# Four neighbouring rows of the down weights on a partition, gate and up columns in steps of four, and an output projection split in two

## The chip, the core and the metric

The kernel runs on one core of a Trainium2 chip. The core has a matrix engine (TensorE, in the profile PE for its matmuls and PEld for its loads of the stationary operand), a vector engine (VectorE, DVE), a scalar engine (ScalarE, ACT), GpSimd (POOL), and SyncE (SP), which in this kernel issues nearly all transfers. Each runs its own list of instructions in order and waits on semaphores for the others. Sixteen DMA engines move data between the chip's memory (HBM) and the on-chip memory (SBUF, 128 partitions); matmuls write to PSUM. The metric is the time of one execution on the device, in microseconds, as the median over several runs.

## What is computed

A trunk of two layers over 256 tokens of width 1024, all in float32. Layer 0 mixes the tokens with a short gated convolution and a stick-breaking attention; layer 1 with a Mamba-2 mixer (inner width 2048, 32 heads, 8 groups). After each of the two, and this is what most of the change touches, comes a mixture of experts: each token chooses one of 4 groups of experts and in it the best 2 of 8, and 32 experts in all work on the tokens that chose them:

```python
def expert_block(args):
    xb, e = args
    hb = jax.nn.silu(xb @ w_gate[e]) * (xb @ w_up[e])
    return hb @ w_down[e]
```

`w_gate[e]` and `w_up[e]` are 1024 x 512, `w_down[e]` is 512 x 1024: 2 MB (2,097,152 bytes) each, 6 MB per expert, 192 matrices in two layers, some 400 MB that must come from HBM once. A final norm follows. The sum over the 512 inner columns in `hb @ w_down[e]` may be taken in any order, as long as column i of `hb` meets row i of `w_down`.

## The kernel before

**The expert loop.** Each expert gets room for 32 tokens (CAP); tokens beyond that go to an overflow pass, here one in layer 1 and none in layer 0. Experts are worked off in fours (QUAD): for each four, `gather_quad` collects the tokens with matmuls (line 1393), and VectorE scales them. For each expert TensorE runs `gate_up` (line 1402), ScalarE and VectorE form silu(gate) x up, TensorE transposes the result (line 1485), `down` (line 1411) multiplies with the down weights, and every four experts `combine_quad` (line 1421) adds their outputs to four PSUM banks (`acc`). `rows_of` (line 1380) spreads the routing for one expert.

In `gate_up` the 32 tokens are the stationary operand, and the weights move through: the 512 columns of gate and up are cut into four blocks, and block j of both (2 x 128 columns) goes to the partitions 32j to 32j+31 of the PSUM tile. Before the change block j is the 128 neighbouring columns from 128j on. After the transposition the inner index within a block lies on the 128 partitions, so `down` wants row 128j + p of `w_down` on partition p, in the j-th place; there the load before puts it, with the access pattern `"a (j p) n -> p (a j) n"` (line 297, and 316 in the overflow pass). On a partition that is four runs of 1024 floats (4 KB) from four places in HBM. The gate and up loads (lines 294 and 313) put 8 neighbouring rows of 512 floats on a partition, one run of 16 KB.

**Order of the loads.** All are issued by SP. There are three sets of weight buffers (`SLOT`); buffers of slot 0, 1 and 2 are `w_gu[s]` and `w_dn[s]`, of which one pair lies in the tiles named w_x and arena in the profile. The first three experts' weights are loaded before the loop. From expert 3 on, `expert_stream` issues gate, up and down of expert e: the gate load waits until `gate_up` of the expert that used the slot last is done (`gu_done`), the down load until its `down` is done (`dn_done`). At expert 28 `overflow_weights` loads the overflow experts' weights, if there are any, and at expert 30 SP waits for the overflow pass to be done.

**The Mamba layer.** It runs over 8 units g. TensorE's order in a unit is `odd_scores(g)`, `odd_z(g)` (projection of z), `odd_y(g)`, `odd_out(g - 2)` (output projection, four PSUM banks b of 8 matmuls each), `odd_x(g + 1)` (projection of x for the next unit), `odd_ss(g)` (sum of squares for the norm), `odd_bc(g + 2)`. For unit 6 the last of these doesn't exist. VectorE's order for a unit is written out too: `odd_mean(g - 1)`, which waits for `odd_ss(g - 1)`; `odd_x_taps(g)`, the convolution of x, which waits for ScalarE's first tap; `odd_mix(g - 1)`; `odd_x_silu(g)`, for which `odd_scores(g)` waits. ScalarE's order is `odd_x_tap(g)`, `odd_rstd(g - 1)`, `odd_x(g)`. `odd_x(g + 1)` on TensorE waits for `z1_silu` of unit g, since both use the PSUM tile pb. The output projection's semaphore `oproj` frees the buffer `w_o` for SP's load of the next unit's output weights (`rows_odd`, lines 280 and 276) and the buffer `mix1` for VectorE.

Of the kernel before, what the change touches and what calls it, by code (L numbers as in the profile page):

```python
# [12 lines left out]
P = 128  # L13
# [5 lines left out]
ODD_UNITS = 8  # L19
# [8 lines left out]
FF = 512  # L28
QUAD = 4
CAP = 32  # L30
OV_AT = 28
OV_SLOT = 1
# [14 lines left out]
def previous(e):  # L47

    return max(i for i in range(e) if SLOT[i] == SLOT[e])
# [36 lines left out]
def trunk_program(nc, x, even_w_in, even_conv_w, even_w_out, odd_in_proj, odd_conv_w, odd_conv_b,  # L86
# [3 lines left out]
    with ExitStack() as ctx:  # L90
        def sb(name, shape, dt=F32):
            return ctx.enter_context(nc.sbuf_tensor(name, shape, dt))
# [12 lines left out]
        w_gu = [sb(f"w_gu{s}", [P, 2, KC, FF]) for s in range(2)]  # L105
        w_dn = [sb(f"w_dn{s}", [P, FF // P, D]) for s in range(2)]
# [78 lines left out]
        mix1 = [take(2, SEQ) for _ in range(2)]  # L185
# [74 lines left out]
        def _(sp_):  # L260
# [27 lines left out]
            def expert_part(l, e, part, after=None):  # L288
                s = SLOT[e]
                if after is not None:  # L290
                    sp_.wait_ge(S["dn_done" if part == 2 else "gu_done"], after + 1)
                w = (expert_w_gate, expert_w_up, expert_w_down)[part][l, ds(e, 1), :, :]
                if part < 2:
                    sp_.dma_start(w_gu[s][:, part], w.rearrange("a (p k) f -> p (a k) f", k=KC)  # L294
                                  ).then_inc((S["gu_in0"], S["gu_in1"], S["gu_in2"])[s], 16)
                else:
                    sp_.dma_start(w_dn[s][:, :, :], w.rearrange("a (j p) n -> p (a j) n", p=P)
                                  ).then_inc((S["dn_in0"], S["dn_in1"], S["dn_in2"])[s], 16)

            def overflow_weights(l):  # L300

                sp_.wait_ge(S["table_done"], l + 1)
                sp_.wait_ge(S["gu_done"], NE * l + previous(OV_AT + 2) + 1)
                sp_.wait_ge(S["dn_done"], NE * l + previous(OV_AT + 2) + 1)
                k0 = sp_.value_load(table[0:1, l:l + 1], min_val=0, max_val=OV_LIST)
                k1 = sp_.value_load(table[0:1, l + 1:l + 2], min_val=0, max_val=OV_LIST)
                with sp_.If(k0 < k1):
                    with sp_.Fori(k0, k1) as k:
                        sp_.wait_ge(S["ov_done"], k + 1)
                        e = sp_.value_load(table[0:1, ds(k + 3, 1)], min_val=0, max_val=NE - 1)  # L310
                        for part in range(2):
                            w = (expert_w_gate, expert_w_up)[part][l, ds(e, 1), :, :]
                            sp_.dma_start(w_gu[OV_SLOT][:, part], w.rearrange("a (p k) f -> p (a k) f", k=KC)
                                          ).then_inc(S["ov_in"], 16)
                        w = expert_w_down[l, ds(e, 1), :, :]
                        sp_.dma_start(w_dn[OV_SLOT][:, :, :], w.rearrange("a (j p) n -> p (a j) n", p=P)
                                      ).then_inc(S["ov_in"], 16)

            def expert_stream(l):
# [824 lines left out]
        def _(pe):  # L1144
            mm = nc.tensor.matmul
# [15 lines left out]
            def project(dst, w, j, used=None):  # L1161

                for k in range(KC):
                    ins = mm(dst, w[:, k, j, :], hnT[:, k, :], start=(k == 0), stop=(k == KC - 1))  # L1164
                return ins
# [8 lines left out]
            def square_sum(a, last=False):  # L1174
                return mm(wa[0:NG + NE + 1, 0:SEQ], esum[:, :], a, start=False, stop=last, skip_group_check=True)

            def out_project(m, u):
                last = u == ODD_UNITS - 1
                w = w_o
                if u == ODD_UNITS - 2:  # L1180
                    pe.wait_ge(S["wo6_in"], 16)
                    w = w_o6
                else:
                    pe.wait_ge(S["wo_in"], (u + 1 - last) * 16)
                for b in range(4):
                    for i in range(2):
                        for j in range(2):
                            ins = mm(acc[:, b, 256 * i:256 * i + 256], w[:, j, 256 * b + P * i:256 * b + P * i + P],  # L1188
                                     m[:, j, :], start=False, stop=False, skip_group_check=True)
                    if last:  # L1190
                        ins.then_inc(S["eo"], 1)
                        if b:
                            logits_of(1, b - 1)
                if not last:
                    ins.then_inc(S["oproj"], 1)

            pe.wait_ge(S["consts_pool"], 1)
# [2 lines left out]
            for t in range(TT):  # L1200
                pe.wait_ge((S["x_in0"], S["x_in1"])[t], 16)
                for b in range(2):
                    for j in range(4):
                        k = 4 * b + j
                        ins = nc.tensor.transpose(BANKS[2 * t + b][:, P * j:P * j + P], squares[:, t, P * k:P * k + P],
                                                  ident[:, :])
# [190 lines left out]
            def gate_up(xb, c0, s, gu, halves=None):  # L1397
                for k in range(KC):
                    if halves is not None and k % (KC // 2) == 0:
                        pe.wait_ge(S["xs_done"], halves + k // (KC // 2) + 1)  # L1400
                    for j in range(4):
                        ins = mm(gu[32 * j:32 * j + 32, :, :], xb[:, k, c0:c0 + CAP], w_gu[s][:, :, k, P * j:P * j + P],  # L1402
                                 start=(k == 0), stop=(k == KC - 1))
                return ins

# [105 lines left out]
            def odd_x(g):  # L1511
                pe.wait_ge(S["c1_in"], g * 16 + 16)
                if g:
                    pe.wait_ge(S["z1_silu"], g)
                project(pb[:, 0:SEQ], w_c[1], 0)
                project(pb[:, SEQ:], w_c[1], 1).then_inc(S["x1_done"], 1)
# [7 lines left out]
            for k in range(KC):  # L1524
                if k % 2 == 0:
                    pe.wait_ge(S["sq_part"], 5 + k // 2)
                ins = mm(wb[0:1, 0:SEQ], esum[:, NG + NE:], hsq[:, k, :], start=(k == 0), stop=(k == KC - 1))
            ins.then_inc(S["ss_done"], 1)
            pe.wait_ge(S["ss_copied"], 1)
            for t in range(TT):  # L1530
                ins = mm(wa[:, t:t + 1], msR[:, P * t:P * t + P], one_c[0:1, :], start=True, stop=True)
            ins.then_inc(S["ss_t"], 1)
            pe.wait_ge(S["rstd"], 2)
            for t in range(TT):
                ins = mm(pb[:, P * t:P * t + P], st[:, 4, t:t + 1].to_broadcast([P, P]), ident[:, :], start=True, stop=True)
# [41 lines left out]
            def odd_ss(g):  # L1577
                pe.wait_ge(S["yz_done"], g + 1)
                for j in range(2):
                    ins = mm(wb[:, 0:SEQ], ones[:, :], sq[:, j, :], start=(j == 0), stop=(j == 1))  # L1580
                ins.then_inc(S["yss_done"], 1)

            def odd_out(g):
                pe.wait_ge(S["mix1_done"], g + 1)
                out_project(mix1[g % 2], g)

            for g in range(ODD_UNITS):
                odd_scores(g)
                odd_z(g)
                odd_y(g)  # L1590
                if g >= 2:
                    odd_out(g - 2)
                if g + 1 < ODD_UNITS:
                    odd_x(g + 1)
                odd_ss(g)
                if g + 2 < ODD_UNITS:
                    odd_bc(g + 2)
# [29 lines left out]
```

## Time and profile before

| | |
|---|---|
| median of 3 runs | 1404.64 us (1402.79 to 1407.19) |
| the profiled execution: time | 1403.31 us |
| its span, first to last instruction | 1401.2 us |
| TensorE matmuls busy | 1093.9 us (78%), 9381 records |
| VectorE / ScalarE busy | 434.8 us (31%) / 262.1 us (19%) |
| read from HBM | 465.68 MB |
| mean granted TensorE clock | 0.869 of full speed |

A float32 matmul shows as two records. Busy shares are averages over stages of different kinds, so the views by stretch say more: the page's slices, the windows, and the chain of waits, which goes back from the last instruction from each step to what released it. A transfer's piece in that chain runs from its issue to its landing, and in between the transfers queued before it are moved too.

### The profile page before, as it was taken

The numbers are of one execution on the slowest core, as the hardware profiler recorded it, in microseconds if no ns is written. First come the engines' busy times: TensorE is split into PE (matmuls) and PEld (weight loads), VectorE is DVE, ScalarE is ACT, GpSimd is POOL, SyncE is SP. The second block draws the span as 40 slices with busy tenths as digits, with TensorE's granted clock in tenths as the row PEclk, the third lists the DMA queues.
The fourth block names the chain that finished last, engine by engine and source line by source line (L and its number), as shares of the span: only waits on it lengthen the run. The fifth ranks groups of instructions, "written<-read, shape, count | busy, mean of one in ns | idle before, by whom it ended". The sixth has DMA issues, their size and how long they took to land.

```text
span 1401.2 us, 21348 instructions
## 1 busy us (share of the span) xinstructions
PE 1093.9 (78%) x9381; PEld 731.6 (52%) x9384; DVE 434.8 (31%) x1098; ACT 262.1 (19%) x621; POOL 6.9 (0%) x28
## 2 busy tenths in 40 slices
PE   8999786677658677679999998878667576676775
PEld 7888543443424244248888887644334242343532
DVE  2241442212212122224655554452112122222123
ACT  2210111111111111113433323211111111111112
POOL 1000000000000000000000000000000000000000
PEclk9999997978879778879999999989788787878878
DMA  9753599999999999954567652469999999999993
GB/s 345 233 221 153 238 420 423 420 420 423 419 420 422 420 420 418 417 181 124 193 225 241 228 193 98 189 265 419 419 423 420 420 423 420 419 422 420 420 410 161
DMA packets 112901, 468.16 MB, mean 334 GB/s; under 512 B 16940, under 2 KB 56104, under 8 KB 96168
## 3 DMA queue, kind: packets, MB, share of 16 engines
q1 hardware_dynamic: 112304, 466.11, 83.4%
q8 instruction: 76, 1.25, 0.4%
q10 hardware_dynamic: 504, 0.67, 0.1%
q14 instruction: 17, 0.14, 0.0%
HBM read 465.68 MB, written 1.08 MB: 333 GB/s over the span
## 4 chain that ended last, share of the span: by engine, by line
PE 40%; issue 36%; DMA 17%; SPq 3%; DVE 2%; ACT 1%; POOL 0%; DVEq 0%; POOLq 0%; ACTq 0%
DMA w_gu<-in_expert_w_up 15%; PE pb L1164 10%; PE pa L1164 7%; PE acc L1188 4%; PE pa L1402 4%; SPq L294 3%; DMA w_x<-in_expert_w_up 2%; PE wa L1402 2%; PE acc L1290 2%; PE wb L1411 2%; PE pb L1393 2%; PE pb L1219 1%; ACT arena L448 1%; PE wa L1171 1%; PE acc L1421 1%
## 5 line engine op out<-in xcount | busy, mean ns | idle before, releaser
L1402 PE MATMUL pa<-w_gu,arena 128*32 128x256 f32 x1536 | 131.2, 516 | 80.4 <-DMA w_gu<-in_expert_w_up 80.4
L959 DVE TENSOR_SCALAR arena<-arena 128x128 f32<-128x128 f32 x64 | 14.5, 227 | 501.6 <-ACT arena L448 501.6
L448 ACT ACTIVATE arena<-wb 32x256 f32<-32x256 f32 (+3 forms) x327 | 116.8, 357 | 230.2 <-PE wb L1485 124.6
L1402 PE MATMUL wa<-w_gu,arena 128*32 128x256 f32 x1344 | 101.2, 468 | 53.6 <-DMA w_gu<-in_expert_w_up 52.0
L1402 PEld LDWEIGHTS pa<-w_gu,arena 128*32 128x32 f32 x1536 | 61.3, 147 | 144.7 <-DMA w_gu<-in_expert_w_up 85.5
L1164 PE MATMUL pb<-hnT,w_x 128*128 128x256 f32 x512 | 113.7, 380 | 2.4 <-DVE arena L999 2.4
L1164 PEld LDWEIGHTS pb<-hnT,w_x 128*128 128x128 f32 x512 | 96.9, 191 | 15.7 <-issue 2.8
L1402 PEld LDWEIGHTS wa<-w_gu,arena 128*32 128x32 f32 x1344 | 49.0, 134 | 99.9 <-DMA w_gu<-in_expert_w_up 54.4
L1393 PE MATMUL pb<-arena,hs 128*128 128x128 f32 x480 | 74.4, 319 | 31.8 <-issue 15.1
L1393 PEld LDWEIGHTS pb<-arena,hs 128*128 128x128 f32 x480 | 68.5, 227 | 45.9 <-issue 41.2
L1411 PE MATMUL wb<-w_dn,arena 128*32 128x256 f32 x1440 | 87.0, 383 | 2.2 <-ACT arena L448 2.2
L1380 PE MATMUL pb<-arena 32*128 32x512 f32 x128 | 73.6, 655 | 6.2 <-DVE arena L897 6.2
L1402 PE MATMUL wa<-w_x,arena 128*32 128x256 f32 x768 | 54.6, 444 | 26.9 <-DMA w_x<-in_expert_w_up 23.7
L448 ACT ACTIVATE arena<-pa 128x128 f32<-128x128 f32 (+1 forms) x40 | 11.6, 298 | 340.5 <-PE pa L1402 316.2
L448 ACT ACTIVATE arena<-arena 128x512 f32<-128x512 f32 (+5 forms) x85 | 51.4, 623 | 75.9 <-DVE arena L1053 24.3
L1402 PE MATMUL pa<-w_x,arena 128*32 128x256 f32 x512 | 40.7, 487 | 30.7 <-DMA w_x<-in_expert_w_up 30.7
L1411 PEld LDWEIGHTS wb<-w_dn,arena 128*32 128x32 f32 x1440 | 45.6, 111 | 35.2 <-issue 3.9
L1421 PE MATMUL acc<-arena 128*128 128x256 f32 x256 | 58.4, 381 | 6.6 <-ACT arena L448 6.6
L960 DVE RECIPROCAL arena<-arena 128x128 f32<-128x128 f32 x64 | 61.0, 953 | 2.2
L1164 PE MATMUL pa<-hnT,w_x 128*128 128x256 f32 x256 | 59.5, 393 | 0.0
L448 ACT ACTIVATE arena<-wa 128x128 f32<-128x128 f32 (+3 forms) x40 | 12.3, 306 | 250.9 <-PE wa L1402 243.5
L920 DVE TENSOR_SCALAR arena<-pb,slot_id 128x256 f32<-128x256 f32 x64 | 30.9, 483 | 87.8 <-PE acc L1421 60.6
(278 smaller groups left out, 1216.0 us busy)
## 6 DMA issues: line engine op xcount, KB each, us to landing
w_dn<-in_expert_w_down SPq DMA_DIRECT2D x45, 2048.0 KB, 27.3
w_gu<-in_expert_w_gate SPq DMA_DIRECT2D x45, 2048.0 KB, 31.5
w_gu<-in_expert_w_up SPq DMA_DIRECT2D x45, 2048.0 KB, 30.6
arena<-in_expert_w_down SPq DMA_DIRECT2D x20, 2048.0 KB, 27.7
w_x<-in_expert_w_gate SPq DMA_DIRECT2D x20, 2048.0 KB, 32.0
w_x<-in_expert_w_up SPq DMA_DIRECT2D x20, 2048.0 KB, 30.5
w_x<-in_odd_in_proj SPq DMA_DIRECT2D x16, 1024.0 KB, 5.4
w_x<-in_odd_in_proj SPq DMA_DIRECT2D x16, 512.0 KB, 5.5
```

Of the source, the lines that this page charges most:

```text
L294: sp_.dma_start(w_gu[s][:, part], w.rearrange("a (p k) f -> p (a k) f", k=KC)).then_inc((S["gu_in0"], S["gu_in1"], S["gu_in2"])[s], 16)
L448: return nc.scalar.activation(*a, **k)
L920: link(v.tensor_scalar(G4[b], B_ps[:, 0:SEQ], slot_id[:, :], None, ALU.is_equal))
L960: link(v.reciprocal(eg, eg))
L1164: ins = mm(dst, w[:, k, j, :], hnT[:, k, :], start=(k == 0), stop=(k == KC - 1))
L1188: ins = mm(acc[:, b, 256 * i:256 * i + 256], w[:, j, 256 * b + P * i:256 * b + P * i + P], m[:, j, :], start=False, stop=False, skip_group ...
L1290: ins = mm(acc[:, b, 256 * i:256 * i + 256], we_o[:, j, 256 * b + P * i:256 * b + P * i + P], mixA[:, j, :], start=(j == order[0]), stop=( ...
L1380: mm(B_ps[:, :], sel, PG, start=True, stop=True).then_inc(S["b_done"], 1)
L1393: ins = mm(xg[:, k, :], hs[:, t, KC // 2 * half + k, :], quad_slots[:, t, :], start=(t == 0), stop=(t == TT - 1))
L1402: ins = mm(gu[32 * j:32 * j + 32, :, :], xb[:, k, c0:c0 + CAP], w_gu[s][:, :, k, P * j:P * j + P], start=(k == 0), stop=(k == KC - 1))
L1411: ins = mm(Y_ps[32 * c:32 * c + 32, :], ht[:, 32 * j:32 * j + 32], w_dn[s][:, j, 256 * b:256 * b + 256], start=(j == 0), stop=(j == 3))
L1421: ins = mm(acc[:, b, 256 * i:256 * i + 256], a, m, start=False, stop=False, skip_group_check=True)
```

## The change

The down weights' load puts four neighbouring rows (4p to 4p+3) on partition p, in the places j = 0 to 3, so that 16 KB of a partition lie together in HBM. To match it, `gate_up` takes for block j the columns j, j+4, j+8, ... instead of 128 neighbours; the moving operand's floats then lie 16 bytes apart. All counts and shapes of instructions stay. Apart from this, in the Mamba layer the output projection that runs in unit 6 (that of unit 4) does bank 0 ahead of the x projection of unit 7 and banks 1 to 3 behind it.

```diff
--- before.py
+++ after.py
@@ -294,7 +294,7 @@
                     sp_.dma_start(w_gu[s][:, part], w.rearrange("a (p k) f -> p (a k) f", k=KC)
                                   ).then_inc((S["gu_in0"], S["gu_in1"], S["gu_in2"])[s], 16)
                 else:
-                    sp_.dma_start(w_dn[s][:, :, :], w.rearrange("a (j p) n -> p (a j) n", p=P)
+                    sp_.dma_start(w_dn[s][:, :, :], w.rearrange("a (p j) n -> p (a j) n", p=P)
                                   ).then_inc((S["dn_in0"], S["dn_in1"], S["dn_in2"])[s], 16)
 
             def overflow_weights(l):
@@ -313,7 +313,7 @@
                             sp_.dma_start(w_gu[OV_SLOT][:, part], w.rearrange("a (p k) f -> p (a k) f", k=KC)
                                           ).then_inc(S["ov_in"], 16)
                         w = expert_w_down[l, ds(e, 1), :, :]
-                        sp_.dma_start(w_dn[OV_SLOT][:, :, :], w.rearrange("a (j p) n -> p (a j) n", p=P)
+                        sp_.dma_start(w_dn[OV_SLOT][:, :, :], w.rearrange("a (p j) n -> p (a j) n", p=P)
                                       ).then_inc(S["ov_in"], 16)
 
             def expert_stream(l):
@@ -1174,7 +1174,7 @@
             def square_sum(a, last=False):
                 return mm(wa[0:NG + NE + 1, 0:SEQ], esum[:, :], a, start=False, stop=last, skip_group_check=True)
 
-            def out_project(m, u):
+            def out_project(m, u, banks=(0, 1, 2, 3)):
                 last = u == ODD_UNITS - 1
                 w = w_o
                 if u == ODD_UNITS - 2:
@@ -1182,7 +1182,7 @@
                     w = w_o6
                 else:
                     pe.wait_ge(S["wo_in"], (u + 1 - last) * 16)
-                for b in range(4):
+                for b in banks:
                     for i in range(2):
                         for j in range(2):
                             ins = mm(acc[:, b, 256 * i:256 * i + 256], w[:, j, 256 * b + P * i:256 * b + P * i + P],
@@ -1191,7 +1191,7 @@
                         ins.then_inc(S["eo"], 1)
                         if b:
                             logits_of(1, b - 1)
-                if not last:
+                if not last and 3 in banks:
                     ins.then_inc(S["oproj"], 1)
 
             pe.wait_ge(S["consts_pool"], 1)
@@ -1399,7 +1399,7 @@
                     if halves is not None and k % (KC // 2) == 0:
                         pe.wait_ge(S["xs_done"], halves + k // (KC // 2) + 1)
                     for j in range(4):
-                        ins = mm(gu[32 * j:32 * j + 32, :, :], xb[:, k, c0:c0 + CAP], w_gu[s][:, :, k, P * j:P * j + P],
+                        ins = mm(gu[32 * j:32 * j + 32, :, :], xb[:, k, c0:c0 + CAP], w_gu[s][:, :, k, j:FF:4],
                                  start=(k == 0), stop=(k == KC - 1))
                 return ins
 
@@ -1580,18 +1580,22 @@
                     ins = mm(wb[:, 0:SEQ], ones[:, :], sq[:, j, :], start=(j == 0), stop=(j == 1))
                 ins.then_inc(S["yss_done"], 1)
 
-            def odd_out(g):
+            def odd_out(g, banks=(0, 1, 2, 3)):
                 pe.wait_ge(S["mix1_done"], g + 1)
-                out_project(mix1[g % 2], g)
+                out_project(mix1[g % 2], g, banks)
 
             for g in range(ODD_UNITS):
                 odd_scores(g)
                 odd_z(g)
                 odd_y(g)
-                if g >= 2:
+                if g == ODD_UNITS - 2:
+                    odd_out(g - 2, (0,))
+                elif g >= 2:
                     odd_out(g - 2)
                 if g + 1 < ODD_UNITS:
                     odd_x(g + 1)
+                if g == ODD_UNITS - 2:
+                    odd_out(g - 2, (1, 2, 3))
                 odd_ss(g)
                 if g + 2 < ODD_UNITS:
                     odd_bc(g + 2)
```

## Rows read from the trace of the kernel before

**Rows 1.** Page, part 2: transfer rate in 40 slices; packets by size.

```profile
GB/s 345 233 221 153 238 420 423 420 420 423 419 420 422 420 420 418 417 181 124 193 225 241 228 193 98 189 265 419 419 423 420 420 423 420 419 422 420 420 410 161
...
DMA packets 112901, 468.16 MB, mean 334 GB/s; under 512 B 16940, under 2 KB 56104, under 8 KB 96168
```

**Rows 2.** Chain of waits, 200 to 610 us: start us, length us, what.

```profile
206.33 30.60 DMA w_gu<-in_expert_w_up
...
575.17 23.80 DMA w_gu<-in_expert_w_up
```

**Rows 3.** Timeline, TensorE, layer 1's first experts: start us, us, engine, line, xrecords.

```profile
921.03 3.66 PE L1402 MATMUL wa<-w_gu,arena 128*32 128x256 f32 x64
...
959.90 0.42 PE L1402 MATMUL wa<-w_gu,arena 128*32 128x256 f32 x4
```

**Rows 4.** Windows: stretch, us, TensorE busy (records), granted clock, DMA share, GB/s.

```profile
177.00:179.00 2.00, 1.70 (x32) 1.00 1.02 412
192.00:194.00 2.00, 0.92 (x4) 1.00 1.03 414
207.00:209.00 2.00, 2.00 (x11) 1.00 1.04 414
222.00:224.00 2.00, 2.00 (x24) 0.50 1.03 412
237.00:239.00 2.00, 2.00 (x20) 0.50 1.02 410
183.00:189.00 6.00, 6.00 (x55) 0.56 1.00 426
198.00:203.00 5.00, 5.00 (x87) 1.00 1.01 426
212.00:218.00 6.00, 4.20 (x58) 1.00 1.01 431
227.00:233.00 6.00, 3.54 (x43) 0.97 1.01 429
242.00:248.00 6.00, 4.92 (x59) 0.93 0.99 418
300.00:550.00 250.00, 174.94 (x1872) 0.80 1.01 420
```

**Rows 5.** Timeline, TensorE, last two experts of layer 1; [wait before].

```profile
1360.13 6.47 PE L1402 MATMUL wa<-w_gu,arena 128*32 128x256 f32 x64 [2.26 <-DMA w_gu<-in_expert_w_up]
...
1375.07 5.83 PE L1402 MATMUL pa<-w_gu,arena 128*32 128x256 f32 x64 [4.75 <-DMA w_gu<-in_expert_w_up]
```

**Rows 6.** Timeline, SP: gate loads of experts 3 and 30 in layer 1.

```profile
924.75 0.34 SPq L294 DMA_DIRECT2D w_gu<-in_expert_w_gate  x1
...
1344.36 0.33 SPq L294 DMA_DIRECT2D w_gu<-in_expert_w_gate  x1
```

**Rows 7.** Line 1402, gate and up products: duration ns min/median/max.

```profile
L1402 PE MATMUL wa<-w_gu,arena x1344: 379/379/637, 159.8 to 1366.2; 128*32 128x256 f32 x192
```

**Rows 8.** Lines 703 and 883, reductions on VectorE: duration ns min/median/max.

```profile
L703 DVE TENSOR_REDUCE arena<-hnT x2: 1979/1980/1981, 131.6 to 897.8; 128x256 f32<-128x1024 f32 x2
...
L883 DVE TENSOR_REDUCE arena<-hnT x2: 1222/1222/1222, 176.5 to 937.8; 128x32 f32<-128x1024 f32 x2
```

**Rows 9.** Timelines around the x projection of unit 7, by engine.

```profile
843.17 7.17 PE L1188 MATMUL acc<-arena,w_x 128*128 128x256 f32 x32
850.18 7.07 PE L1164 MATMUL pb<-hnT,w_x 128*128 128x256 f32 x32
857.09 1.03 PE L1580 MATMUL wb<-arena,ones 128*128 128x256 f32 x4
...
857.29 1.02 ACT L448 ACTIVATE arena<-pb,vec_cols,conv_cols_sb 128x256 f32<-128x256 f32 x2 [6.80 <-PE pb L1164]
...
858.15 0.42 DVE L1096 TENSOR_SCALAR arena<-wb 128x256 f32<-128x256 f32 x1 [9.27 <-PE wb L1580]
...
864.37 1.19 PE L1559 MATMUL wa<-arena 128*128 128x256 f32 x2 [6.25 <-DVE arena L1017]
```

## The prediction

> **What bounds the kernel now.** I read the page's slices of DMA rate first. In slices 6 to 17 and again in 28 to 39 the transfers run at 410 to 423 GB/s, and between them, in the Mamba layer, at about half of that [rows 1]. The two flat stretches are the two expert loops. Then the chain of waits: through an expert loop it is, every three experts, one piece of some 30.5 us that stands for weight transfers, with a few us of TensorE before it; the last such piece of layer 0 ends at 599.0 [rows 2]. So each loop is bound by the stream of weights, three loads of 2.097 MB per expert. TensorE follows: four experts without a wait take 38.9 us (921.03 to 959.90, [rows 3]), while their twelve loads take 12 x 2.097 MB / 420 GB/s = 59.9 us [rows 4]. It waits for the gate and up weights before nearly each expert, and the last wait of layer 1 is 4.75 us before the gate-up product at 1375.07 [rows 5]. The Mamba layer is bound by TensorE and by the chain of vector and scalar work between its products, not by transfers.
>
> **Part 1, the down weights.** Before, a partition's 16 KB of a down load are four runs of 4 KB from four places in the tensor. After, they are one run of 16 KB, as the gate and up loads have always been. What a packet costs at either size follows from windows that lie within one kind of load. DMA share and GB/s there count the same packets, so their ratio, times 16 engines, times the packet's bytes, is the mean duration of a packet, and it doesn't depend on where the window cuts. Five windows within down loads (the first five rows, one per expert, 15 us apart): 1.02/412, 1.03/414, 1.04/414, 1.03/412, 1.02/410, mean 0.002493; times 16 x 4096 B: 163.4 ns for 4 KB. Five within gate and up loads (the next five): 1.00/426, 1.01/426, 1.01/431, 1.01/429, 0.99/418, mean 0.002357; times 16 x 16384 B: 617.8 ns for 16 KB [rows 4]. Each of 16 engines fills 8 partitions: a down load costs it 32 x 163.4 = 5.229 us, a gate load 8 x 617.8 = 4.943 us. The change turns the first into the second: 0.286 us less per down load.
>
> How many of these lie on the path? Layer 1: the first load of the loop is issued at 924.75, the last up load has landed at 1375.07 [rows 5, 6]; in between run 60 gate and up loads (experts 3 to 31 and one overflow expert) and 29 down loads (experts 3 to 30 and the overflow expert; that of expert 31 comes behind the last up load). 60 x 4.943 + 29 x 5.229 = 448.2 us, against 450.3 measured: about 2 us for the first bytes and the last receipt, so there is no gap to fill, and any saving of a packet moves the end. Layer 0 has no overflow expert: 28 down loads. Sum: 57 x 0.286 = 16.3 us. Bounds: the plain rates of the same windows are 412.4 and 426.0 GB/s, 5.085 and 4.923 us, 0.162 per load, which is 9 us. Upwards, the two steadiest gate windows (431 and 429) as the rate of the whole stream against its 420 give 2.3% of 885 us, 20 us: rates dip at the borders between the two kinds of load, and those borders lose their reason. I take 16.3, since the ratio is free of the cut and its sum meets the measured length.
>
> The page "DMA: Bandwidth & Descriptors" of the Trainium skill, section "Why small descriptors are slow", puts a fixed overhead of about 3 cycles on a packet. An estimate from that: 4 x (128 + 3) against 512 + 3 beats, 1.7% of a down load, 5 us for the 57. The trace shows 5.5% between the sizes, and the measurement decides.
>
> What is late next? Still the stream: an expert's three loads then need 14.8 us, TensorE 38.9 / 4 = 9.7. At the end the last down load must be there when expert 31's product wants it; it lands one load behind the last up load, some 5 us, and the gate-up product (5.83, [rows 5]) and the transpose come first. The place where TensorE could take over is the overflow expert of layer 1: expert 30's gate and up loads are issued at 1344.36 [rows 6] when it is finished, and used at 1360.13 [rows 5], 15.8 us later; two loads take 9.9 and about 1.5 for the latency, so about 4.4 us of older loads were still queued. The three down loads of that stretch take 0.9 of it. 3.5 remain, so the whole saving passes.
>
> **Part 2, gate and up columns in steps of four.** Per gate-up product the number, shapes and stationary tiles of the matmuls stay; only the moving operand now takes every fourth float (16 bytes apart) where it took neighbours. No matmul of the trace before reads its moving operand so. What the rows show: 64 records of 379 ns in 3.66 us [rows 3, 7], so one every 52 ns ((3.66 - 0.38) / 63), on four column tiles side by side. Below, nothing excludes a small gain, but nothing offers one: 0. Above, the nearest reading of floats that aren't neighbours is VectorE's: the reduction of 1024 elements with a step of 1 KB takes 1.98 us, one over 1024 neighbours 1.22, a ratio of 1.62 [rows 8]. The far bound is a fetch of 16 bytes for each float instead of for four: a ratio of 4. I take 1.0: with four tiles side by side a tile has 4 x 52 = 208 ns for the 256 floats of a record, 0.8 ns for each, which leaves two clocks for a float at the granted clock of 1.0 (2.4 GHz), and a slower reading is hidden up to a point: four products may grow by 59.9 - 1.1 - 38.9 = 19.9 us in all, a ratio of 1 + 19.9 / 14.6 = 2.36, before TensorE sets the pace.
>
> What isn't hidden at a ratio r: the first gate-up product of each layer (the first refill waits for it, 3.66 x (r - 1)); the last one of each layer, which starts when its weights land (5.83 us at the lower clock: from hardly anything, if the reading takes a fixed time that the slow pace covers, to 5.83 x (r - 1)); and in layer 1 the two products before the overflow expert is done (the same bounds each, less the 3.5 us above). At 1.62: 4.5 + 0.2 to 7.2 + 0 to 3.7, so 5 to 15 us, middle 10. At 2: 7.3 + 0 to 11.7 + 0 to 8.2, middle 17.
>
> The page "SBUF — State Buffer" of the Trainium skill, section "Specifications", speaks against this edit: lines are 16 bytes, full bandwidth needs at least two hits per line, and each access that crosses to a new line pays. With neighbours a line is hit four times, with the new step once. By that rule the ratio is above 1; it gives no size. It is the rule behind the second and third case below; no row here shows a matmul under it.
>
> **Part 3, the output projection of unit 4 split around the x projection of unit 7.** In the stretch before, the projection takes 7.1 us from 843.17, the x projection runs from 850.18, the sum of squares of unit 6 from 857.09, and then TensorE waits 6.25 us until 864.37 [rows 9]. With one bank of four ahead, the x projection starts at about 845.0 and ends at 851.9, 5.3 us earlier; ScalarE's first tap (857.29 before) follows it. But VectorE's next instruction is the mean of unit 6, at 858.15, released by the sum of squares; the taps of unit 7 stand behind it in VectorE's order, and the scores wait for those. The sum of squares keeps its place behind all four banks, at 857.1, so the mean, the taps and the scores come when they came. Gain 0. Cost: the semaphore that frees the output weights rises 7 us later, at 857.2, so SP's load of unit 5's output weights and, queued behind it, that of unit 6's start 7 us later; they are wanted only after the scores of unit 7 and a z projection of 7 us, behind 871, and a load of that size takes some 5. Behind those in SP's queue stands expert 2's gate load, which waits for the z projection of unit 7 anyway. 0, with 0.2 us either way for one more change of tile on TensorE.
>
> **Sum.** 16.3 + 0 + 0. From the profiled execution's own 1403.3 us (span 1401.2 and 2.1 around it) to 1387.0; that execution lies 1.3 us under the median of 1404.64, so the median to be expected is 1388.3.
>
> **The rivals.** (B) The strided reading costs about what VectorE's does: ratio 1.62, 10 us back, 1398. For it: the row and the rule. Against: another engine, a step of 1 KB, and TensorE's pace per float is slower. (C) The other side: the reading becomes the bound of the gate-up product, ratio 2 to 4. At 2 it gives back 17 us, 1405, which is the point from which the change is a loss. Beyond 2.36 TensorE paces the loop. At 4 a product takes 14.6 us, four experts 82.8 instead of 58.8, over some 15 such groups in both layers +360, and the time is about 1750. For it: four column tiles read at once, 256 floats each, and each float on a line of its own. Against: none of the rows shows reading as TensorE's limit. (D) The packets don't matter: the down loads are limited by what they read or write, and the stream stays at 420 GB/s; 1404.6. Against: two kinds of load, same bytes per partition, same source speed, differ by packet size alone in what the trace shows. (E) The split works: the scores of unit 7 come up to 5.3 us earlier, 1383. Only if VectorE's order weren't what holds them.
>
> **Chances.** Forecast 0.57, B 0.14, C 0.15, D 0.10, E 0.04. A measurement of this kernel can tell about 0.3% (4.2 us) from no change. Faster: 0.565 + 0.13 + 0.02 of C near 2 + 0.02 of D + 0.04 = 0.77. Same: 0.005 + 0.01 + 0.01 + 0.07 = 0.10. Slower: 0.12 of C and 0.01 of D, 0.13. The range runs from 1382 (the 20 us bound of part 1 and a little) to 1405 (B's whole width, C at 2, and most of D); it leaves out C beyond 2.
>
> **What would show it.** Right: the page counts about 65 x 384 = 25,000 fewer packets, those of 8 KB and more grow from 16,733 (112,901 - 96,168, [rows 1]) to some 25,000; rate slices of the loops rise from 420 to about 427; pieces of about 30.5 us in the chain shrink to about 30, gate-up products stay at 3.66 us where nothing interrupts them; the scores of unit 7 keep their 6 us wait. Wrong in part 2: gate-up products of 5.9 us or 7 and more at the full clock, or the wait for weights gone and the rate slices below 420. Wrong in part 1: fewer packets and the same 420. Wrong in part 3: TensorE's wait before the scores of unit 7 at about 1 us.

## Result, and the profile after

The changed kernel takes 1413.38 us (median of 9 runs, 1411.29 to 1417.86) against 1404.64 us before (9 runs, 1402.38 to 1407.33): 0.67% slower, ratio 1.0067 with a 95% interval of 1.0052 to 1.0082. Forecast were 1388.3 us and a range from 1382 to 1405. One execution of E9 below took 1515.01 us at a mean granted clock of 0.704, where the other five took 1380.75 to 1382.84, and is left out of its ratio.

The page after, answering to [rows 1]: span; TensorE; granted clock in tenths and transfer rate in 40 slices of 35.3 us; packets.

```profile
span 1410.8 us, 21349 instructions
...
PE 1251.8 (89%) x9381; PEld 735.3 (52%) x9384; DVE 434.7 (31%) x1098; ACT 262.2 (19%) x621; POOL 6.9 (0%) x28
...
PEclk9999899999899998989999999999999999999899
...
GB/s 344 237 211 155 193 405 427 427 428 426 427 427 427 427 427 415 386 179 143 188 240 233 227 173 110 191 201 427 428 427 426 427 428 426 427 426 427 429 359 143
DMA packets 87940, 468.14 MB, mean 332 GB/s; under 512 B 16940, under 2 KB 56104, under 8 KB 62888
```

The load's part did what it should: 25,000 packets fewer, and the slices of the expert loops stand at 426 to 429 GB/s where they stood at 417 to 423. But the rate sags at the loops' first slices (193 and 405, against 238 and 420) and last ones (386 and 359, against 417 and 410), and TensorE is busy for 1252 us instead of 1094. The gate-up products, answering to [rows 7], and two windows inside one such product each, one at the full granted clock (1.00, 2.4 GHz) and one at the lower (0.50, 1.2 GHz):

```profile
L1402 PE MATMUL wa<-w_gu,arena x1344: 612/632/676, 160.8 to 1378.8; 128*32 128x256 f32 x192
...
L1402 PE MATMUL pa<-w_gu,arena x1536: 616/632/672, 170.8 to 1389.9; 128*32 128x256 f32 x192
```
```profile
420.90:424.30 3.40, 3.38 (x32) 0.50 1.00 424
301.90:309.00 7.10, 7.10 (x64) 1.00 1.01 432
```

Every record now takes 632 ns, at least 612, where it took 379 in the stretches of full clock; and the granted clock no longer matters: 32 records touch 3.4 us of the slow window, 64 touch 7.1 us of the fast one, about the same pace. Before, durations of some 634 ns stood at the lower clock alone (the records that touch 222.0 to 224.0, at 0.50). A product of 64 records takes 7.43 us, where it took 3.66 at the full clock, a ratio of 2.03; behind a wait for weights, where the clock before was partly at its lower level, it took 4.96 to 6.62 and now takes 7.43 to 7.58 too.

Where that reaches the end: the last experts of layer 1 in the timeline of TensorE, answering to [rows 5], and SP's first refills of layer 0.

```profile
1350.67 7.43 PE L1402 MATMUL wa<-w_x,arena 128*32 128x256 f32 x64
...
1360.86 7.50 PE L1402 MATMUL pa<-w_gu,arena 128*32 128x256 f32 x64
...
1371.98 7.43 PE L1402 MATMUL wa<-w_gu,arena 128*32 128x256 f32 x64
...
1383.06 7.45 PE L1402 MATMUL pa<-w_gu,arena 128*32 128x256 f32 x64
```
```profile
168.33 0.33 SPq L294 DMA_DIRECT2D w_gu<-in_expert_w_gate  x1
168.70 0.43 SPq L294 DMA_DIRECT2D w_gu<-in_expert_w_up  x1
180.04 0.33 SPq L297 DMA_DIRECT2D w_dn<-in_expert_w_down  x1
```

No product waits for weights at the end: the starts are 11.1 us apart (1360.86, 1371.98, 1383.06), which is TensorE's own pace for one expert. The stream no longer bounds the last four experts (28 to 31; the overflow expert comes before them). At the start the first refill is issued when the first product is done (160.83 + 7.43), and the second only at 180.04, 11.7 us later, while the two loads of the first take about 10.

The first window below, within the second wait of SP, shows the transfers running dry; two long windows in the middle show the full rate:

```profile
179.00:182.00 3.00, 2.39 (x27) 1.00 0.71 213
300.00:550.00 250.00, 211.62 (x1877) 0.92 1.00 426
1000.00:1250.00 250.00, 218.04 (x1919) 0.92 1.01 427
```

The Mamba stretch, answering to [rows 9]:

```profile
847.40 7.07 PE L1164 MATMUL pb<-hnT,w_x 128*128 128x256 f32 x32
...
859.49 1.03 PE L1580 MATMUL wb<-arena,ones 128*128 128x256 f32 x4
866.77 1.19 PE L1559 MATMUL wa<-arena 128*128 128x256 f32 x2 [6.25 <-DVE arena L1017]
```
```profile
860.55 0.42 DVE L1096 TENSOR_SCALAR arena<-wb 128x256 f32<-128x256 f32 x1 [9.28 <-PE wb L1580]
```

The x projection now starts at 847.40, behind one bank of the output projection (845.57) instead of four, and the wait before the scores of unit 7 is 6.25 us, to the digit what it was: VectorE's mean at 860.55 is still released by the sum of squares at 859.49.

### The profile page after: what moved, and what is told of

Its sections match the earlier page's. It is cut to its first block, busy times and chain, and to the rows that moved or that the text cites. A ratio compares the mean times of both kernels' runs of the same rounds, so it can differ in the third digit from the quotient of the medians.

```text
span 1410.8 us, 21349 instructions
## 1 busy us (share of the span) xinstructions
PE 1251.8 (89%) x9381; PEld 735.3 (52%) x9384; DVE 434.7 (31%) x1098; ACT 262.2 (19%) x621; POOL 6.9 (0%) x28
## 4 chain that ended last, share of the span: by engine, by line
PE 48%; issue 36%; DMA 11%; DVE 2%; ACT 2%; SPq 0%; POOL 0%; DVEq 0%; POOLq 0%; ACTq 0%
PE pb L1164 10%; PE pa L1164 7%; DMA w_gu<-in_expert_w_up 7%; PE wa L1402 6%; PE pa L1402 6%; DMA w_x<-in_expert_w_up 4%; PE acc L1188 4%; PE wb L1411 3%; PE pb L1393 3%; PE acc L1290 2%; ACT arena L448 2%; PE pb L1219 1%; PE acc L1421 1%; PE wa L1171 1%; PE pb L1380 1%
## 5 line engine op out<-in xcount | busy, mean ns | idle before, releaser
L1402 PE MATMUL pa<-w_gu,arena 128*32 128x256 f32 x1536 | 179.4, 633 | 21.2 <-DMA w_gu<-in_expert_w_up 21.2
L1402 PE MATMUL wa<-w_gu,arena 128*32 128x256 f32 x1344 | 156.3, 632 | 7.1 <-DMA w_gu<-in_expert_w_up 5.6
L1402 PEld LDWEIGHTS pa<-w_gu,arena 128*32 128x32 f32 x1536 | 56.6, 130 | 126.1 <-issue 102.7
L1402 PE MATMUL wa<-w_x,arena 128*32 128x256 f32 x768 | 90.4, 631 | 13.2 <-DMA w_x<-in_expert_w_up 11.3
L1411 PEld LDWEIGHTS wb<-w_dn,arena 128*32 128x32 f32 x1440 | 50.0, 115 | 50.0 <-issue 27.8
L448 ACT ACTIVATE arena<-pa 128x128 f32<-128x128 f32 (+1 forms) x40 | 11.6, 299 | 324.1 <-PE pa L1402 299.8
L1402 PE MATMUL pa<-w_x,arena 128*32 128x256 f32 x512 | 59.6, 632 | 7.6 <-DMA w_x<-in_expert_w_up 7.4
L1402 PEld LDWEIGHTS wa<-w_x,arena 128*32 128x32 f32 x768 | 27.6, 129 | 67.0 <-issue 54.6
```

The lines of the kernel that those rows point to most:

```text
L448: return nc.scalar.activation(*a, **k)
L1411: ins = mm(Y_ps[32 * c:32 * c + 32, :], ht[:, 32 * j:32 * j + 32], w_dn[s][:, j, 256 * b:256 * b + 256], start=(j == 0), stop=(j == 3))
```

## Experiments

**E1, the down load alone.** Edit, in both load functions:

```diff
-w.rearrange("a (j p) n -> p (a j) n", p=P)
+w.rearrange("a (p j) n -> p (a j) n", p=P)
```

> The kernel before with the new access pattern of the down load alone (four neighbouring rows on a partition, packets of 16 KB); gate and up columns stay neighbours, so the hidden columns don't meet their rows and the output is another one; the instructions are the same. Theory: the changed kernel lost by TensorE's reading alone, and the load's gain is there in full: packets of 617.8 ns for 16 KB in place of four of 163.4, 57 down loads on the path, 16 us faster, about 1388; gate-up products stay at 3.66 us. Rival: the larger packets bring little by themselves (the 5 us of a fixed overhead per packet), about 1400.

Measured: 1377.27 us against 1404.29, ratio 0.9803 (0.9785 to 0.9821): 27 us, more than either theory gives. The reason is in the page's issues of this kernel:

```profile
w_dn<-in_expert_w_down SPq DMA_DIRECT2D x44, 2048.0 KB, 26.3
```

44 and not 45: with other values out of layer 0, layer 1 routes its tokens otherwise, and its overflow pass doesn't happen, which carries a load of 6.3 MB and a stop of the loop with it. Layer 0 has no such pass in any kernel, so its length (start of the first gate-up product to start of the sum of squares of line 1527) can be compared: 160.21 to 610.99, 450.8 us, against 159.80 to 616.86, 457.1. The load is worth 6.3 us in layer 0. Layer 1, from its first product to the end of the span, takes 459.5 us against 480.2.

**E2, the step of four alone.**

```diff
-w_gu[s][:, :, k, P * j:P * j + P]
+w_gu[s][:, :, k, j:FF:4]
```

> The kernel before with gate and up columns in steps of four alone; the down load stays at four runs of 4 KB, so the output is another one. Theory: the step doubles each gate-up product (7.4 us instead of 3.66), and what of it isn't hidden costs what the load's gain and the loss of the whole change add up to, 16 + 9 = 25 us: about 1430. Rival: the load brought only 5 us, then the step costs 14: about 1418.

Measured: 1402.68 us, ratio 0.9987 (0.9978 to 0.9997), where 1430 and 1418 were expected. It looks free, but it lacks the overflow pass too. Layer 0: 159.51 to 623.53, 464.0 us, 7.0 more than before.

**E3, the split alone.** The two edits of the diff at `out_project` and `odd_out`, and the loop.

> The kernel before with the output projection of unit 4 split around the x projection of unit 7, as in the changed kernel, and nothing else. Theory: no difference (within 1 us of 1404.6), since VectorE's mean of unit 6 still waits for the sum of squares behind all four banks; TensorE's wait before the scores of unit 7 stays at 6.2 us. Rival: the later release of the output weights or a slower clock behind it costs 2 us or more.

Measured: 1404.47 us, ratio 1.0000 (0.9991 to 1.0010). The theory holds: nothing, and in its trace TensorE's wait before the scores of unit 7 is 6.25 us.

**E4, a step of two.**

```diff
-w_gu[s][:, :, k, P * j:P * j + P]
+w_gu[s][:, :, k, 256 * (j // 2) + j % 2:256 * (j // 2) + 256:2]
-w_dn[s][:, :, :], w.rearrange("a (j p) n -> p (a j) n", p=P)
+w_dn[s][:, :, :].rearrange("p (c b) n -> p c (b n)", b=2),
+w.rearrange("a (c p b) n -> p (a c) (b n)", c=2, b=2)
```

> The kernel before with a middle layout that computes the reference: two neighbouring rows (8 KB) in each of two runs on a partition, gate and up columns in steps of two (8 bytes apart, two floats of each 16-byte line). Theory A, the line decides: with two floats used per line a gate-up product takes 3.66 us as before, packets of 8 KB take 315 ns (between the two sizes on a line), 0.19 us per down load, 11 us faster, about 1394. Theory B, any step above one slows the reading: products of 7.4 us, some 14 us slower, about 1418. In between (a product of 4 to 6 us) the step's bytes set the rate.

Measured: 1397.21 us, ratio 0.9944 (0.9927 to 0.9960): 7 us faster. The two costliest gate-up groups in its lines (busy us, mean ns of a record), a window of the loop, and the first product of layer 0 in the timeline:

```profile
L1404 PE MATMUL pa<-w_gu,arena 128*32 128x256 f32 x1536 | 131.6, 512 | 80.8 <-DMA w_gu<-in_expert_w_up 80.8
...
L1404 PE MATMUL wa<-w_gu,arena 128*32 128x256 f32 x1344 | 101.9, 466 | 46.6 <-DMA w_gu<-in_expert_w_up 44.9 <-DVE arena L937 1.6
```
```profile
300.00:550.00 250.00, 178.46 (x1879) 0.81 1.01 424
```
```profile
159.59 3.83 PE L1404 MATMUL wa<-w_gu,arena 128*32 128x256 f32 x64
```

Means of 512 and 466 ns, against 516 and 468 for the same groups before (both levels of the clock mixed) and 632 with the step of four. The means hide a small price: at the full clock a product takes 3.83 us instead of 3.66, 5% more, and a record 385 to 391 ns instead of 379. So theory A holds nearly: with two floats used of each 16 bytes the reading is almost at full pace. The stream runs at 424 GB/s, between 420 and 427, as its packets of 8 KB lie between; the gain is 7 us and not the 11 expected, 3.6 in layer 0 (453.5 us) and 3.4 in layer 1 (476.8).

**E5 and E6, each half in layer 1 alone**, so that the routing of layer 1 stays what it is (the condition `l == 1` around the edits of E1 and E2).

> Layer 0 as before; in layer 1 the new down load alone with neighbouring gate and up columns (the hidden columns of layer 1 don't meet their rows, so only the output's values change: routing, and with it the one overflow pass, are those of the reference, which was not so in the two kernels that did this in both layers). Theory: layer 1 gains 29 x 0.286 = 8 us less what its edges keep, 6 to 8 us, about 1397.5. Rival: the two kernels with changed values owed their times to the layer's loads, not to the missing overflow pass; then this gains 17 us or more.

Measured: 1400.30 us, ratio 0.9960 (0.9946 to 0.9974), 5.3 us faster than the 1405.62 of the runs of before beside it. Layer 1, from its first product to the end of the span, takes 474.1 us (922.63 to 1396.7) against 480.2 (921.03 to 1401.2): 6.1 us, as the theory has it. The lengths of layers are compared and not the spans, since stretches with the same instructions can differ by 2 us between two traces: the Mamba layer takes 306.4 us in those of E5 and E6 and 304.2 in that of before.

> Layer 0 as before; in layer 1 gate and up columns in steps of four alone, the down load as before (only the output's values change, routing and overflow pass are the reference's). Theory: the products of 7.4 us cost at the edges of the loop (first refill, overflow pass, last experts) 10 to 15 us, about 1417. Rival: the step alone is free, as the kernel with it in both layers seemed to say (1402.7 against 1404.3), about 1404.

Measured: 1414.13 us, ratio 1.0065 (1.0051 to 1.0080), 8.5 us slower; layer 1 takes 489.8 us (922.22 to 1412.0), 9.6 more than before. The step costs; in E2 the missing overflow pass made up for it. 8.5 us is under the 10 to 15 expected.

The end of layer 1 in E5, to lay beside that of the changed kernel:

```profile
1295.73 5.74 PE L1402 MATMUL pa<-w_gu,arena 128*32 128x256 f32 x64 [4.72 <-DMA w_gu<-in_expert_w_up]
...
1355.76 6.43 PE L1402 MATMUL wa<-w_gu,arena 128*32 128x256 f32 x64 [6.14 <-DMA w_gu<-in_expert_w_up]
...
1370.40 5.95 PE L1402 MATMUL pa<-w_gu,arena 128*32 128x256 f32 x64 [4.49 <-DMA w_gu<-in_expert_w_up]
```

Here the last two products wait 6.1 and 4.5 us for their weights.

**E7, the step in the middle only** (the condition, shortened).

```diff
+step = 4 <= e <= 20   # layer 1; else neighbours, down load as in E5
```

> As the kernel with the new down load in layer 1 alone, but experts 4 to 20 of layer 1 take their gate and up columns in steps of four (only the output's values change). Theory: in the middle of the loop a product of 7.4 us is hidden behind the 14.8 us of an expert's loads, so this takes what that kernel takes, within 1.5 us. Rival: the step costs everywhere, 17 of 33 products, some 7 us more than that kernel.

Measured: 1399.99 us, ratio 0.9962 (0.9948 to 0.9975), the same as E5. Expert 31's product in its trace:

```profile
1369.30 5.42 PE L1402 MATMUL pa<-w_gu,arena 128*32 128x256 f32 x64 [7.34 <-DMA w_gu<-in_expert_w_up]
```

It starts 448.0 us after the layer's first (921.32), in E5 447.8. So seventeen products with the step, 7.43 to 7.58 us each, cost nothing in the middle of the loop; what E6 and the changed kernel lose, they lose at the loop's two ends. (The rest, from there to the end of the span, is 2 us longer in this trace than in E5's, another difference of the kind named above.)

**E8, VectorE turns the blocks.** Neighbouring columns again for TensorE, new down load, and (shortened)

```diff
-v.tensor_tensor(hb, eg, GU[e % 2][:, 1, :], ALU.mult).then_inc(S["h_done"], 1)
+v.tensor_tensor(hb.rearrange("p (q m) -> p m q", q=4), eg.rearrange("p (m q) -> p m q", q=4),
+    GU[e % 2][:, 1, :].rearrange("p (m q) -> p m q", q=4), ALU.mult).then_inc(S["h_done"], 1)
+dve.wait_ge(S["h_done"], E + 1)
+dve.wait_ge(S["dn_done"], E)
+v.transpose(hT, hb).then_inc(S["ht_copied"], 1)
```

TensorE's transposition and ScalarE's copy of it are gone, in the overflow pass too. The block of 32 x 32 that stays on its 32 partitions is enough, since column 128j + 4p + i of the hidden layer is wanted on partition 32j + p.

> The changed kernel with neighbouring gate and up columns again; the hidden columns are brought to their rows of the down weights by VectorE instead: it writes silu(gate) x up with its columns in steps and turns it in blocks of 32 x 32 straight into the stationary operand, which also takes away TensorE's transposition and ScalarE's copy. It computes the reference. Theory: the load's gain without TensorE's price: 1404.3 less 13 to 16 and some 1 us at each loop's end, about 1389. Rival: VectorE's two instructions are slow in this form (over 1.5 us more per expert) or the new wait holds it up; then above 1392.

Measured: 1388.92 us, ratio 0.9882 (0.9867 to 0.9897). VectorE's new instruction:

```profile
L965 DVE STREAM_TRANSPOSE arena<-arena 128x128 f32<-128x128 f32 x64 | 19.9, 311 | 2.2
```

0.31 us per expert, and the multiplication with its strided operands 0.37 instead of 0.29. So this kernel has the changed kernel's load and leaves TensorE its contiguous reading. It is 16.7 us faster than the 1405.62 beside it; layer 0 takes 449.5 us and layer 1 473.2, 1.3 and 0.9 less than with the load alone (E1, E5), near the 1 us per loop's end that was expected for the work taken away.

**E9 and E10, the sum of squares ahead of banks 1 to 3**, on top of E8 and on the kernel before:

```diff
 if g == ODD_UNITS - 2:
     odd_out(g - 2, (0,))
 ...
     odd_x(g + 1)
+odd_ss(g)
 if g == ODD_UNITS - 2:
     odd_out(g - 2, (1, 2, 3))
-odd_ss(g)
```

> The kernel before with the split and the sum of squares ahead of banks 1 to 3, nothing else. Theory: 4 to 5 us faster, about 1400, TensorE's wait before the scores of unit 7 about 1.5 to 2 us instead of 6.25. Rival (the split itself brings nothing for another reason than the place of the sum of squares): 1404.5.

Measured: 1397.86 us, ratio 0.9955 (0.9943 to 0.9968), 6.5 us faster than before. TensorE, and VectorE's mean, in E10:

```profile
842.51 1.99 PE L1188 MATMUL acc<-arena,w_x 128*128 128x256 f32 x8
...
851.25 1.03 PE L1580 MATMUL wb<-arena,ones 128*128 128x256 f32 x4
...
859.15 0.67 PE L1559 MATMUL wa<-arena 128*128 128x256 f32 x2 [1.69 <-issue]
...
860.31 7.07 PE L1164 MATMUL pb<-hnT,w_x 128*128 128x256 f32 x32
```
```profile
852.31 0.42 DVE L1096 TENSOR_SCALAR arena<-wb 128x256 f32<-128x256 f32 x1 [4.09 <-PE wb L1580]
```

Counted from the start of the output projection (842.51 here, 843.17 in [rows 9]), the mean comes after 9.8 us instead of 15.0 and the scores after 16.6 instead of 21.2: 4.6 us, as expected. TensorE waits 1.7 us instead of 6.25, and that gives more: from the scores to the z projection it takes 1.2 us instead of 2.3 (864.37 to 866.63 before), and the projection 7.07 instead of 7.52, both since in the kernel before the granted clock behind the long wait was at its lower level for a while (0.50 from 864.3 to 866.6, 0.94 on average from 866.6 to 874.0), while in E10 it is 1.00 from 859.1 to 867.4. Together 6.1 of the 6.5 us.

> The kernel with VectorE's block transposition, and in unit 6 of the Mamba layer the sum of squares moved ahead of banks 1 to 3 of the output projection, right behind the x projection of unit 7. It computes the reference. Theory: VectorE's mean of unit 6 is what held the taps of unit 7; now it comes some 5.3 us earlier, less 0.6 because the release of mix1 by the fourth bank becomes the last thing waited for: 4 to 5 us faster than the kernel with the block transposition alone (1388.9), about 1384.5. Rival: the taps are held by something else; then 1388.9.

Measured: 1382.45 us, ratio 0.9846 (0.9833 to 0.9859): 22 us under the kernel before and 31 under the changed one, the best version found, which computes the reference. Under E8 it is 6.5 us, where 4 to 5 were expected; as in E10, TensorE's wait before the scores is 1.69 us.

**E11 and E12, what the step costs by itself.** E11: a step of eight, `.rearrange("p g (i b j) -> p g b i j", b=2, j=4)[:, :, :, :, j]` on the gate and up columns. E12: `hnT[:, k, :].rearrange("p (m q) -> p q m", q=4)` as the moving operand of the z projections.

> The kernel before with gate and up columns in steps of eight (32 bytes), two interleaved runs of 64 per block, so that each float lies on a 16-byte line of its own and every other line is skipped; the output's values change, so only the products' durations count. Theory: one line per float is what costs, not the distance: 7.4 us per product and records of 632 ns, as with steps of four. Rival: the distance matters (places that are busy again sooner), then 10 us or more.

> The kernel before, but the z projections of the Mamba layer (full 128 x 128 stationary tiles, no column tiles side by side) read their 256 tokens in steps of four; the output's values change, so only these products' durations count. Theory A, each stream of a tile is slowed by itself: the 465 ns that a record with a step takes per tile in the expert loop stand against the 216 ns between records of a projection, so a projection goes from 6.9 to some 14.9 us. Theory B, four streams side by side share a limit of one line per 0.45 ns: a single stream stays below it and a projection stays at 6.9 us.

One run each, for the durations (E11 took 1405.32 us, without an overflow pass, E12 1462.59). The gate-up products of E11, and a z projection of E12 in TensorE's timeline:

```profile
L1402 PE MATMUL wa<-w_gu,arena x1280: 624/641/652, 159.1 to 1367.8; 128*32 128x256 f32 x183
```
```profile
714.12 7.07 PE L1165 MATMUL pa<-hnT,w_x 128*128 128x256 f32 x32
...
722.11 14.60 PE L1165 MATMUL pb<-hnT,w_x 128*128 128x256 f32 x32
```

E11: 641 ns per record, 7.57 us per product (159.14 in its timeline): the distance hardly matters, the line does. E12: 14.60 us for 32 records beside 7.07 for as many without the step (714.12): theory A. A stream of one tile is slowed by itself: with the last record's own 0.63 or 0.38 us taken off, a record starts every 451 ns ((14.60 - 0.63) / 31) instead of every 216 ((7.07 - 0.38) / 31), 1.8 ns for each of 256 floats. In the changed kernel the 64 records of a product are 16 rounds over the four column tiles, and a round starts every 453 ns ((7.43 - 0.63) / 15): four streams side by side take as long as one and don't disturb one another.

## Why the prediction was wrong

**The step that failed** is the choice "I take 1.0" for the ratio of a strided to a contiguous gate-up product. It is 2.03. The prediction had case C for it, with 1405 at a ratio of 2, and the range ended there.

That choice rested on 0.8 ns, two clocks, for each float of a tile, and on "TensorE's pace per float is slower" than VectorE's. The rows could not carry this: they gave the pace of reading neighbours, and nothing on the time that a float on a line of its own takes. E4, E11 and E12 give it: with two floats used of each 16 bytes a product takes 5% more at the full clock, with one it takes 1.8 ns for each float at either clock, and this for every stream by itself. The page "SBUF — State Buffer" of the Trainium skill, section "Specifications", says it: "need ≥2 hits per line for full bandwidth". By that rule steps of four pay and steps of two don't, and the runs agree in the main: at the full clock 7.43 us per product with four, 3.83 with two, 3.66 with neighbours. The prediction named this rule as speaking against the edit and then weighed it below an argument from pace that no row showed.

The right ratio would not have been enough: with it the prediction's own sum gives 1405. Of the other 8 us the edges are 3.8 (20.8 measured, 17 reckoned) and the load 3.9 (12.4 measured, 16.3 reckoned).

**The hidden part was right, its edges were not complete.** E7 shows a doubled product free in the middle, as reckoned. (The 38.9 us of "four experts without a wait" do hold a wait of 3.1 us for VectorE before 943.10 and a product of 5.58 us, so TensorE has a little more slack there than was reckoned.) For the edges at a ratio of 2 the prediction had 7 to 27 us, middle 17. Its lower end has a slip: a last product of 7.3 us is 1.5 longer than one of 5.83 even if the reading takes a fixed time, 3 us for both layers, where the sum has 0. Measured against a kernel with the same loads and a ratio of 1 (E1 for layer 0, E5 for layer 1):

| start of, in us after the layer's first product | layer 0, E1 | layer 0, changed | layer 1, E5 | layer 1, changed |
|---|---|---|---|---|
| expert 27's product | 373.3 | 379.1 | 373.1 | 379.4 |
| expert 31's product | 433.3 | 440.0 | 447.8 | 457.9 |
| end (line 1527; span) | 450.8 | 460.1 | 474.1 | 485.6 |

So layer 0 loses 9.3 us, 5.8 by expert 27, 0.9 between 27 and 31, 2.6 behind; layer 1 loses 11.5, 6.3 by expert 27, 3.8 between, 1.4 behind. The first refill, 3.7 us late, was in the sum. The second wasn't: it is issued 11.7 us after the first instead of 7.9, the transfers run dry, and another 2 us are gone, in either layer. The issues in E1, and its transfer rate as long after the first product as the 213 GB/s above:

```profile
163.93 0.33 SPq L294 DMA_DIRECT2D w_gu<-in_expert_w_gate  x1
...
171.86 0.33 SPq L297 DMA_DIRECT2D w_dn<-in_expert_w_down  x1
```
```profile
178.40:181.40 3.00, 0.70 (x16) 1.00 0.97 410
```

In the first 30 us of layer 0 the changed kernel gets 271 GB/s and E1 352: 2.4 MB, or 5.7 us of the stream, and in the 330 us behind them both get 427, so nothing more is lost there. Nor was it seen that behind expert 28 the products follow one another at TensorE's pace. In layer 1 the overflow expert's product and expert 28's take 15.4 and 10.2 us to the next one's start, against 11.6 and 6.3 in E5; the waits of 6.1 and 4.5 us for weights that E5 still has before experts 30 and 31 give most of that back.

**The load's gain** was taken as 16.3 us and is 12.4: 6.3 in layer 0 (E1), 6.1 in layer 1 (E5). The term that was too large is the 163.4 ns per packet of 4 KB. A share above 1, as the 1.02 to 1.04 in [rows 4], means that durations of packets overlap on an engine, so a packet's duration isn't the time that it takes from the stream; the windows of 16 KB packets stood at about 1.00. That this is the whole reason is argued, not shown. The plain rates of the long windows give it better: 420 before, 427 after, 1.6% of 885 us, 14 us; the lower bound of the prediction, from the plain rates of the short ones, was 9, and why the two differ stays open.

The estimate from the page "DMA: Bandwidth & Descriptors" of the Trainium skill, section "Why small descriptors are slow", 5 us, is too small: E1 and E5 show 12.4.

**The split** brought 0 (E3), for the reason given: VectorE's order. E10 moves the one instruction that the reason names and gets the 6.5 us.

**The sum again.** 20.8 us lost, 12.4 won, 8.4; the spans differ by 9.6, of which 1.0 lies ahead of the first product of layer 0 (159.80 against 160.83), where no edit touches anything and the traces of the experiments lie between 158.66 and 160.21, and 0.1 in the Mamba layer. The medians differ by 8.7.

**A trap in the experiments.** E1 and E2 seemed to say that each half alone is a gain (27 and 2 us) and only both together a loss. That was the routing: values out of layer 0 decide the work of layer 1. The overflow pass is worth some 14.6 us there (layer 1 takes 459.5 in E1 and 474.1 in E5), and 17.1 with the step (472.7 in E2, 489.8 in E6). An experiment that changes values has to keep those on which the amount of work depends; E5 and E6 do.

## What to carry to other kernels

Price an access pattern before a layout: in float32 a moving operand that uses every second float cost 5% at the full clock, one that uses a single float of each 16 bytes halved TensorE's pace there. An engine with slack in the middle of a stream has none at its ends in a loop like this one, where the first refills and the last products follow its own pace: sum the edges, every refill until the queue is full again. And when an instruction is moved ahead to release a chain, look in the waiting engine's own order for what stands ahead of the freed one; here the sum of squares, not the x projection, had to move.

## What the runs showed of the hardware beside it

With contiguous reading a gate-up product goes by the granted clock, with steps of four by a fixed time. Counted from the starts of the records in the traces, a round of four records begins every 216 ns before at 2.4 GHz and every 427 at 1.2, with steps of two every 227 and 427, with steps of four every 453 at both levels: twice as long at the full clock, 6% longer at the lower. So the mean granted clock rose from 0.869 to 0.945 with nothing gained: TensorE's matmuls are busy for 89% of the span instead of 78%. VectorE's block transposition of 128 x 128 floats took 0.31 us, less than the 0.33 + 0.28 us of TensorE's transposition and ScalarE's copy before.
